# A tensor of TensorE operands moved by 64 bytes in a two-block transformer kernel

## The reference, cut to what matters

```python
def swiglu(x, w_in, w_out):          # D_FF = 2816, D_MODEL = 1024
    gu = x @ w_in
    g, u = gu[..., :D_FF], gu[..., D_FF:]
    return (jax.nn.silu(g) * u) @ w_out
x = layer_norm(ALPHA * x + 0.5 * swiglu(x, ffn_w_in[l, 0], ffn_w_out[l, 0]), ln_g[l, 0], ln_b[l, 0])
```

## Time and profile before

| | |
|---|---|
| median of 3 runs | 3288.99 us (3288.38 to 3290.56) |
| profiled execution, its own time | 3290.32 us |
| its span, first to last instruction | 3288.5 us |
| mean granted TensorE clock | 0.994 |
| TensorE matmul busy | 3197.6 us, 97% |
| VectorE, ScalarE busy | 65%, 47% |
| 128x256 matmuls with `tz` moving | 3 lines x 1728 |
| 128x256 matmuls with `xh`, `xl` moving, lines 792 to 794 | 3 lines x 1296 |
| 128x512 matmuls with `tz` stationary | 3 lines x 1056 |

### The profile page before, as it was taken

The page is one execution under the profiler, slowest core; times in us unless marked ns, Lnnn a source line. Parts: engine busy times, 40 slices in busy tenths (PEclk is TensorE's granted clock), DMA queues, the critical chain, the costliest instruction groups (busy, mean ns, idle before and its releaser), DMA issues. The chain is left out here.

```text
span 3288.5 us, 55994 instructions
## 1 busy us (share of the span) xinstructions
PE 3197.6 (97%) x22750; PEld 2829.6 (86%) x22750; DVE 2144.5 (65%) x3383; ACT 1534.5 (47%) x2651; POOL 136.3 (4%) x144
## 2 busy tenths in 40 slices
PE   9999999999999999999999988999999989999999
PEld 8998888899889988768998776779998767789987
DVE  6875544787577766447875766557774665567863
ACT  4553444355434543553554544444554444444553
POOL 0000111000000001000000100000000000000000
PEclk9999999999999999999999999999999999999999
DMA  4443222234323432112343221113442221123332
GB/s 177 133 141 114 94 71 86 79 129 144 122 86 114 141 117 98 52 65 84 129 142 117 89 77 59 34 65 112 133 142 96 97 65 53 40 87 113 139 125 71
DMA packets 104512, 331.55 MB, mean 101 GB/s; under 512 B 11264, under 2 KB 16640, under 8 KB 104256
## 3 DMA queue, kind: packets, MB, share of 16 engines
q1 hardware_dynamic: 104256, 327.96, 29.7%
HBM read 325.69 MB, written 2.23 MB: 100 GB/s over the span
## 5 line engine op out<-in xcount | busy, mean ns | idle before, releaser
L219 DVE TENSOR_TENSOR wlo<-raw,whi 128x1024 fp32r<-128x1024 f32 x319 | 388.0, 1225 | 441.7 <-ACT whi L211 441.2
L211 ACT ACTIVATE whi<-raw 128x1024 fp32r<-128x1024 f32 x319 | 334.0, 1054 | 391.2 <-PE ps L369 338.6
L792 PE MATMUL ps<-tz,whi 128*128 128x256 f32 x1728 | 479.9, 278 | 3.4 <-ACT tmp L964 3.4
L793 PE MATMUL ps<-tz,whi 128*128 128x256 f32 x1728 | 478.5, 277 | 0.0
L794 PE MATMUL ps<-tz,wlo 128*128 128x256 f32 x1728 | 477.7, 276 | 0.0
L369 PE MATMUL ps<-whi,tz 128*128 128x512 f32 x1056 | 416.0, 394 | 0.0
L368 PE MATMUL ps<-wlo,tz 128*128 128x512 f32 x1056 | 413.8, 392 | 0.0
L367 PE MATMUL ps<-whi,tz 128*128 128x512 f32 x1056 | 411.3, 390 | 0.0
L794 PE MATMUL ps<-xh,wlo 128*128 128x256 f32 x1296 | 365.7, 282 | 0.0
L792 PE MATMUL ps<-xh,whi 128*128 128x256 f32 x1296 | 365.3, 282 | 0.0
L793 PE MATMUL ps<-xl,whi 128*128 128x256 f32 x1296 | 364.3, 281 | 0.0
(11 more groups left out here) (348 smaller groups left out, 6417.9 us busy)
## 6 DMA issues: line engine op xcount, KB each, us to landing
raw<-in_w SPq DMA_DIRECT2D x535, 512.0 KB, 4.0
fb<-in_w SPq DMA_DIRECT2D x108, 256.0 KB, 2.6
rows<-in_row SPq DMA_DIRECT2D x15, 512.0 KB, 4.9
xr<-in_xt SPq DMA_DIRECT2D x4, 512.0 KB, 6.8
xr<-in_x SPq DMA_DIRECT2D x1, 2048.0 KB, 7.8
mn<-bounds SPq DMA_DIRECT2D x8, 256.0 KB, 4.4
out<-tmp SPq DMA_DIRECT2D x4, 256.0 KB, 3.0
out<-rows SPq DMA_DIRECT2D x4, 256.0 KB, 2.3
```

Source lines behind the costliest of these rows:

```text
L211: a.activation(self.whi[u % NW][:, :], self.raw[u % NRAW][:, :], COPY).then_inc(*self.up("whi", u))
L219: v.tensor_tensor(self.wlo[u % NW][:, :], self.raw[u % NRAW][:, :], f32(self.whi[u % NW][:, :]), SUB).then_inc(*self.up("wlo", u))
L792: t.matmul(out, fh[:, sl], xh[:, k, :], start=first and k == 0, stop=False, skip_group_check=not first)
L793: t.matmul(out, fh[:, sl], xl[:, k, :], start=False, stop=False, skip_group_check=not first)
```

## The change

`tz` is allocated behind a pad of 16 numbers a partition (64 bytes), and a second pad follows it. `tz` then starts at a multiple of 128 bytes, `es` and `fb` start 128 bytes further than before and so stand as they did against a multiple of 128, and `hf` stays. No instruction is added, removed or reordered, and nothing reads or writes the pads.

```diff
         with ExitStack() as scope:
-            hf, tz = c.sb("hf", [P, KF, T], F32, scope), c.sb("tz", [P, 8, 2 * T], F32R, scope)
+            hf = c.sb("hf", [P, KF, T], F32, scope)
+            c.sb("pad0", [P, 16], F32, scope)
+            tz = c.sb("tz", [P, 8, 2 * T], F32R, scope)
+            c.sb("pad1", [P, 16], F32, scope)
             es, fb = c.sb("es", [P, 3, HK], F32, scope), c.sb("fb", [P, 2 * HK], F32, scope)
```

## The result

The changed kernel takes 3318.49 us (median of 4 runs, 3314.95 to 3319.27), the kernel before 3288.68 us beside it: a ratio of 1.0088, 95% interval 1.0071 to 1.0106. It is 29.8 us slower; 3316 was forecast.

A forecast was written before the change was run, and what follows sets the result against it. The prediction took TensorE, busy 97% of the span, to bound the kernel. Its terms, +32 us (`tz` moving), -5 us (stationary) and 0 for the rest, gave +27 and 3316 us; range 3284 to 3325, likeliest case alone 3306 to 3325.

The forecast's parts named there:

- What bounds the kernel: Whole kernel: TensorE, busy 97% of the span; in the FFN products the other engines wait for it.
- Token forms as moving operand: FFN products 4 to 7: moving `tz` goes from 113.5 to `xh`'s 120.0 ns a matmul, +32 us.
- the 17 matmuls: Sign in the FFN products: 17 with `tz` moving behind a run of `xh` take 2.04 us instead of 1.93.
- The sum by stages: FFN products: 1488 matmuls at 120.0 ns plus 0.56 us idle, 179.1 us, +5.3; six FFNs 32.4 us.
- The sum by single matmuls: FFN products with `tz` moving: 5184 x (120.0 - 113.5) = 33.7 us.
- Split activations as stationary operand: FFN output products: stationary `tz` gains 1.6 ns on each of 3168 matmuls, -5 us.
- Writes and the rest: VectorE's and ScalarE's writes and reads of `tz` run beside TensorE; pads and other tensors cost nothing: 0 us.
- the two waits that were shown: Sign in the FFN products: VectorE's and ScalarE's waits for TensorE grow by about 5 us together.
- line 792's duration: Sign in the FFN products: this line's duration with `tz` goes from 278 to some 283 ns.
- A: Rival: the address does not matter; 3289 us, or 3284 if only the stationary part follows it; chance 0.15.
- B: Rival: alignment speeds up the 5184 moving `tz` streams; 3249 us, or 3269 at half of it; chance 0.08.
- C: Rival: moving `tz` takes 120 ns and stationary `tz` loses 1.5 to 3 ns; 3326 to 3330 us; chance 0.06.

The follow-up runs named there:

- e3: Before with `tz` allocated ahead of `hf`, 45056 bytes nearer to `xh`, at the same start modulo 128: 3288.4 us.
- e2: Before with `whi` and `wlo` 64 bytes further between two pads, which move everything behind them, `tz` too, by 128 bytes: 3308.74 us.
- e7: Before with a pad of 32 numbers ahead of `tz`, so `tz` 128 bytes further, at 64 modulo 256: 3328.01 us.
- e11: Before with `tz` 192 bytes further, at 128 modulo 256 from `whi`: 3323.09 us.
- e4: Before with `xh` and `xl` 64 bytes further between two pads, which also put `tz` 128 bytes further: 3275.5 us.
- e8: e4 with the second pad 128 bytes longer, so `tz` is back at 192 modulo 256 and `xh` stays at 64: 3306.67 us.
- e5: After with the two uses of `tz` parted: token forms at 64 modulo 256, split activations at 0: 3308.15 us, ratio 1.0054 to before.
- e9: Before with `xh` and `xl` put at 192 modulo 256, where `tz` also stands: 3269.16 us, ratio 0.9937.
- e10: e9 with the two uses of `tz` parted, token forms at 192 modulo 256 and split activations at 0: 3258.85 us, ratio 0.9915.
- e12: e9 with `tz` 128 bytes further, at 64 modulo 256: 3313.12 us.
- e6: e5 with e4's edit too: `xh` and `xl` at 64 modulo 256, token forms at 192, split activations at 128: 3312.55 us, ratio 1.0069.

## Why the prediction was right

**What bounds the kernel.** Held. The three paces of TensorE's matmuls give the differences of all the kernels to within some 4 us.

**Token forms as moving operand, +32 us.** Right in size. The stretch grew by 5.6 us an FFN (5.3 forecast), 33.8 us in six with the last two products, and the 17 matmuls took the 2.04 us that were named. `xh`'s pace was the right price: in after the two tensors cannot be told apart. The sum by stages is 2 us low. It counts 1488 matmuls in 173.80 us, where there are 1489 in 173.88, and it adds the 0.56 us in which TensorE idles, where the wait costs 0.80 us from start to start. The sum by single matmuls, 33.7 us, hits the total with two errors that cancel: of the measured 33.8 only 29.9 are `tz`'s, whose mean in before was 114.2 and not 113.5 ns, and 3.9 are those of the first `xh` and `xl` matmuls behind each switch, whose mean went from 119.0 to 120.0.

**Split activations as stationary operand, -5 us.** Right in sign and near in size, -6.3: 3168 x (228.9 - 226.9). The rows used showed a gain of 1.3 ns, and the 1.6 that was taken went beyond them by a guess; the mean over all in before was 228.9. As said below, the sign hung on luck.

**Writes and the rest, 0.** Right; 685 and 616 ns, where they were 685 and 617.

**The range and the signs.** Two of its sums do not come out: the full gain of 9 us in the output products gives 3289 + 32 - 9 = 3312, not 3306, and no gain with all of 33.7 lost gives 3323, not 3325. The measured 3318.5 lies inside either way. Of the signs, the two waits that were shown grew by 3.7 us together, where 5 were named, and line 792's duration is 284 ns, where 283 was.

**Rivals.** A fell by e3 (another place, same pace) and by e2 beside e7 (same place, other pace). The Trainium skill, "SBUF — State Buffer", section "SBUF: two separate sides", says TensorE waits on no one there and has an independent read port for the weight load. Two independent reads do not agree with these runs, where the pace of a 128x256 matmul moves by up to 6.5 ns in 120 with the distance between the two operands' starts; that another engine holds TensorE up, no run here shows.

B fell by after itself. C did not come, but its size is real: e7 and e11, with `tz` at 64 and 128 modulo 256, are 38 and 33 us slower than before, and lose in the output products too. Its reason, the order of the slots, is not the cause: the order is the same in all, and the output products follow the start.

The prediction also held its 113.5 and 120.0 ns against a formula. The Trainium skill, "TensorE: Matmul & The Clock Gate", section "Back-to-back issue gap", gives that formula for an isolated matmul and says that in a stream of weight loads and matmuls both set the spacing. So these paces, each with its weight load, are no test of it.

**What failed is the mechanism's wording, not a term.** "How the two stand to each other modulo 128 bytes": the first half holds by e2 beside e7, and by the check behind the table. The second is too coarse. Between 0 and 64 modulo 128 it told 120.0 from less, but not 113.4 from 117.8, nor 227 from 232 for the stationary operand. That the forecast came out all the same is in part luck. It asked for the place where `xh` already stood, to which the trace had a row, but it counted that place modulo 128 only. `tz` stood at 192 modulo 256, so the pad brought it to 0, where `xh` is. e11 brings it to 128, the same place modulo 128, and there the output products take 232.4 ns: the term of -5 us would have been +11. The expectations of e2 and of e4 to e8, which left the measured places, missed by 20 to 59 us.

**Left open.** Whether the weight load and the moving columns meet in SBUF at all, as the prediction took it; only the dependence on the two starts is shown. What picks between 113.4 and 117.8 ns: a switch from `xh` at 0 led to 113 with `tz` at 192 (before, e3) and to 118 at 64 (e5, e7), in all six FFNs of each profiled execution, while e9 went both ways with one set of addresses. And whether 32, 96 and 128 bytes have paces of their own for the moving stream, or are mixed: at 128 (e11) the single distances run from 115 to 122 ns.

## What to carry to other kernels

The start of an SBUF tensor is a tuning knob: print where the operands of the dense matmuls lie modulo 256, read the distance between starts for each pair of moving and stationary tensor, and try pads of 64 bytes. Round numbers are not best: with the moving tensor in step with the weights, a 128x256 float32r matmul was at its slowest here, while at 512 columns it was at its fastest. Moving and stationary uses of one buffer can be given their own starts; e10 gained by it and e5 lost, so every combination has to be timed, more than once where runs scatter. Move one tensor at a time, since a pad shifts all that is allocated behind it.

## What the runs showed of the hardware

- A 128x256 float32r matmul in a dense stream with a weight load for each takes 120.0 ns at 2.4 GHz where the moving tensor and the weights start alike modulo 256 (after; `tz` in e2), 113.4 or 117.8 ns where they are 64 or 192 bytes apart (before, e2 to e10, e12), and 118.7 ns on average at 128 (e11).
- A 128x512 one costs 227, 233, 232 or 229 ns with the stationary tensor 0, 64, 128 or 192 bytes modulo 256 behind the moving one, the same in every kernel that had the place (`tz` at 0: after, e2, e5, e10; 64: e4, e7, e12; 128: e6, e11; 192: before, e3, e8, e9) and, for 0, 64 and 192, with `xh` in either role.
- At 64 or 192 bytes the addresses do not fix the pace of the moving stream: 175.96 and 169.79 us for one stretch of code on one set of addresses in one execution of e9, whose runs scatter over 16 us where those of before beside it scatter over 3.
- Moving `tz` by 45056 bytes, a multiple of 256, did nothing (e3: 479.9 us for line 792, as in before).
